# High halves of the activations straight from the transposes' bank; the first unit of a stage multiplied contraction block by contraction block

## The reference

```
h = x * (1.0 + sc_m) + sh_m          # per column scale and shift
z = h @ w_in                         # even / odd mixer: 1024 x (thousands)
x = layer_norm(ALPHA * x + (1.0 + g_m) * y, ...)
h = x * (1.0 + sc_f) + sh_f
u = causal_dwconv(h @ w_up, conv_w)  # w_up: 1024 x 5632
y = (silu(gate) * val) @ w_down
```

## Time and profile before

| what | value |
|---|---|
| median of 3 runs | 1254.31 us (1252.47 to 1254.63) |
| profiled execution, its own time | 1247.78 us |
| its span, first to last instruction | 1245.7 us |
| TensorE busy | 1155.2 us (93%), mean granted clock 0.965 |
| GpSimd busy | 827.4 us (66%) |
| ScalarE busy | 582.8 us (47%) |
| VectorE busy | 559.4 us (45%) |

### The profile page before, as it was taken

One profiled execution on the slowest core, in us unless ns is written; L12 is line 12 of the kernel. 1 busy time (PEld: TensorE's weight loads), 2 busy tenths in 40 slices (PEclk: granted clock), 3 DMA queues, 4 the chain that ended last, 5 costly groups with the idle time before them and its releaser, 6 DMA issues.

```text
span 1245.7 us, 21662 instructions
## 1 busy us (share of the span) xinstructions
PE 1155.2 (93%) x8119; PEld 1043.1 (84%) x8119; DVE 559.4 (45%) x1149; ACT 582.8 (47%) x868; POOL 827.4 (66%) x290
## 2 busy tenths in 40 slices
PE   6899798999999876999999989999999998999996
PEld 2799687999996873989999959999998987999995
DVE  4359666766557886375322372224211234111113
ACT  0443525554542435354554515455777543554452
POOL 3567448988882730689888825656565765988884
PEclk9899989999998988999999998999999998999998
DMA  9788567999984350678655523444444553666661
GB/s 342 262 292 231 187 209 233 345 335 320 301 301 151 98 136 1 220 227 263 202 179 175 170 65 93 144 135 137 136 139 136 187 165 103 194 192 183 188 185 67
DMA packets 253193, 237.69 MB, mean 191 GB/s; under 512 B 18043, under 2 KB 216496, under 8 KB 253136
## 3 DMA queue, kind: packets, MB, share of 16 engines
q1 hardware_dynamic: 237312, 202.80, 52.6%
q10 hardware_dynamic: 14784, 31.98, 7.1%
q0 software_dynamic: 1040, 2.12, 0.5%
HBM read 235.83 MB, written 1.05 MB: 190 GB/s over the span
## 4 chain that ended last, share of the span: by engine, by line
PE 72%; DVE 8%; ACT 7%; POOL 5%; DMA 5%; issue 2%; SPq 0%; DVEq 0%; POOLq 0%; ACTq 0%
PE bank L1147 18%; PE bank L1148 18%; PE bank L1149 18%; POOL unit_lo L688 5%; ACT unit_hi L790 3%; DMA raw<-in_ev_w_in 2%; PE bank L1186 2%; PE bank L1172 2%; PE bank L1174 2%; PE bank L1218 2%; PE bank L1206 1%; DMA att<-in_ada_w 1%; PE bank L1208 1%; PE bank L1226 1%; PE bank L1327 1%
## 5 line engine op out<-in xcount | busy, mean ns | idle before, releaser
L688 POOL TENSOR_TENSOR unit_lo<-raw,unit_hi 128x2048 fp32r<-128x2048 f32 (+4 forms) x88 | 349.3, 3973 | 261.0 <-ACT unit_hi L790 260.9
L1147 PE MATMUL bank<-h_hi,unit_hi 128*128 128x256 f32 x1248 | 354.2, 284 | 0.3
L1148 PE MATMUL bank<-h_lo,unit_hi 128*128 128x256 f32 x1248 | 353.5, 283 | 0.0
L1149 PE MATMUL bank<-h_hi,unit_lo 128*128 128x256 f32 x1248 | 353.4, 283 | 0.0
L722 POOL TENSOR_TENSOR unit_lo<-raw,unit_hi 128x2048 fp32r<-128x2048 f32 (+1 forms) x70 | 257.2, 3675 | 70.5 <-ACT unit_hi L922 66.9
L1147 PEld LDWEIGHTS bank<-h_hi,unit_hi 128*128 128x128 f32 x1248 | 239.6, 192 | 5.0 <-issue 1.3
L1148 PEld LDWEIGHTS bank<-h_lo,unit_hi 128*128 128x128 f32 x1248 | 239.6, 192 | 2.7
L1149 PEld LDWEIGHTS bank<-h_hi,unit_lo 128*128 128x128 f32 x1248 | 239.6, 192 | 0.0
L790 ACT ACTIVATE unit_hi<-raw 128x2048 fp32r<-128x2048 f32 (+4 forms) x98 | 163.2, 1666 | 105.9 <-PE bank L1149 38.0
L725 POOL TENSOR_TENSOR down<-raw_down,down 128x1024 fp32r<-128x1024 f32 x70 | 176.2, 2517 | 0.0
L1862 DVE SCALAR_TENSOR_TENSOR work<-bank,cols,work 128x254 f32<-128x254 f32 (+1 forms) x176 | 72.7, 474 | 146.9 <-ACT work L909 146.9
(11 more groups left out here) (310 smaller groups left out, 2065.1 us busy)
## 6 DMA issues: line engine op xcount, KB each, us to landing
raw<-in_ffn_w_up SPq DMA_DIRECT2D x88, 512.0 KB, 5.2
raw<-in_w_in SPq DMA_DIRECT2D x60, 512.0 KB, 4.6
raw_down<-in_ffn_w_down SPq DMA_DIRECT2D x44, 512.0 KB, 4.9
raw<-in_w_up SPq DMA_DIRECT2D x64, 256.0 KB, 3.1
raw_down<-in_w_down SPq DMA_DIRECT2D x32, 512.0 KB, 3.5
raw<-in_ev_w_in SPq DMA_DIRECT2D x28, 512.0 KB, 5.3
ada<-in_ada_w ACTq DMA_DIRECT2D x13, 1024.0 KB, 7.8
att<-in_ada_w SPq DMA_DIRECT2D x12, 1024.0 KB, 7.7
```

Source lines behind the costliest of these rows:

```text
L688: nc.gpsimd.tensor_tensor(ul[g % 2][:, w], raw[g % 2][:, w], uh[g % 2][:, w].bitcast(F32), ALU.subtract).then_inc(lo_up, 1)
L1147: nc.tensor.matmul(o, sh, mh, start=first, stop=False)
L1148: nc.tensor.matmul(o, sh, ml, start=False, stop=False)
L1149: return nc.tensor.matmul(o, sl, mh, start=False, stop=last)
```

## The change

- ScalarE writes hh directly from the banks, one kt block at a time, in the order 0 to 7, and counts `h_hi` up after each. It no longer touches hf. For the odd quarters it waits until VectorE has read the bank.
- VectorE writes hf of all four quarters, in the order 1, 0, 3, 2; for the even ones it waits until ScalarE has read the bank. It then subtracts only quarter 3 (in stage 0 all four, as before).
- GpSimd subtracts the quarters 0, 1 and 2, in that order, each behind VectorE's hf and ScalarE's hh. Its queue is otherwise unchanged.
- `first_units` multiplies the first unit of a stage block by block: for each kt, as soon as its hh is there, all column blocks (or row blocks) with the high and the low half of the weights; then for each kt the hl products. It waits for the unit's low half before it starts, except in stage 0 (`low_last`), where the low half comes last. In stage 4 it takes `G_F` and the first query unit together, in stage 5 the first two feed-forward blocks together.
- `keep_warm(8)` ahead of stage 2's transposes becomes `keep_warm(5)`.

```diff
             def h_low(n):
-                for q in (0, 2):
-                    pool.wait_ge(h_hi, 4 * n + q + 1)
+                for q in range(3):
+                    evacuated(pool, ("ht", n, q))
+                    pool.wait_ge(h_hi, KD * n + 2 * q + 2)
                     k = slice(2 * q, 2 * q + 2)
                     nc.gpsimd.tensor_tensor(hl[:, k, :], hf[:, k, :], hh[:, k, :].bitcast(F32), ALU.subtract
-                                            ).then_inc(h_lo[0], 1)
+                                            ).then_inc(h_lo_pool, 1)
...
             def h_high(n, columns, scale, shift):
                 evacuated(act, columns)
-                def whole(q):
+                for q in range(4):
                     o = full(act, ("ht", n, q))
+                    if q % 2:
+                        evacuated(act, ("ht", n, q))
                     for i in range(2):
                         kt = 2 * q + i
-                        dst, src = hf[:, kt, :], o[:, S * i:S * (i + 1)]
+                        dst, src = hh[:, kt, :], o[:, S * i:S * (i + 1)]
...
-                    ins.then_inc(free(("ht", n, q)), 1)
-                def high(q):
-                    evacuated(act, ("ht", n, q))
-                    k = slice(2 * q, 2 * q + 2)
-                    nc.scalar.activation(hh[:, k, :], hf[:, k, :], ACT.Copy).then_inc(h_hi, 1)
-                whole(1)
-                high(0)
-                high(1)
-                whole(3)
-                high(2)
-                high(3)
+                        ins.then_inc(h_hi, 1)
...
+            def h_low_ready(n, kt):
+                q = kt // 2
+                if n == 0:
+                    pe.wait_ge(h_lo_dve, q + 1)
+                elif q < 3:
+                    pe.wait_ge(h_lo_pool, 3 * (n - 1) + q + 1)
+                else:
+                    pe.wait_ge(h_lo_dve, 4 + n)
+
+            def first_units(n, gs, rows=False, low_last=False):
+                parts = []
...
+                if not low_last:
+                    for g in gs:
+                        pe.wait_ge(lo_up, g + 1)
...
+                for kt in range(KD):
+                    pe.wait_ge(h_hi, KD * n + kt + 1)
+                    for part in parts:
+                        multiply(part, kt, uh, hh, start=kt == 0 and part[3] == 0)
+                        if not low_last:
+                            multiply(part, kt, ul, hh)
+                for kt in range(KD):
+                    h_low_ready(n, kt)
+                    for part in parts:
+                        last = kt == KD - 1 and not low_last
+                        mm = multiply(part, kt, uh, hl, stop=last and ends(part))
+                        if last:
+                            final(part, mm)
+                if low_last:
+                    for g in gs:
+                        pe.wait_ge(lo_up, g + 1)
+                    for kt in range(KD):
+                        for part in parts:
+                            mm = multiply(part, kt, ul, hh, stop=kt == KD - 1 and ends(part))
...
-                up(0, 0, ready=h_ready((1, 3, 5)[f]), high=h_high_ready((1, 3, 5)[f]))
-                up(0, 1)
+                if f < 2:
+                    first_units((1, 3)[f], [g0])
+                    up(0, 1)
+                else:
+                    first_units(5, [g0, g0 + 1])
                 downward(0, 0, True, False)
...
-            for g in G_QI:
-                unit_cols(g, hh, hl, ready=h_ready(0), high=h_high_ready(0))
+            first_units(0, G_QI[:1], low_last=True)
+            unit_cols(G_QI[1], hh, hl)
...
-            keep_warm(8)
+            keep_warm(5)
             transpose_rows(2, x, 3)
-            for g in G_Z:
-                unit_rows(g, hh, hl, ready=h_ready(2), high=h_high_ready(2))
+            first_units(2, G_Z[:1], rows=True)
+            for g in G_Z[1:]:
+                unit_rows(g, hh, hl)
...
-            unit_cols(G_F, hh, hl, blocks=(0,), ready=h_ready(4), high=h_high_ready(4))
+            first_units(4, [G_F, G_QKV[FOX][0]])
             for j, g in enumerate(G_QKV[FOX]):
+                if j == 0:
+                    continue
...
             def h_columns(n, scale, shift):
-                for q in (0, 2):
-                    whole(q)
-                for q in (0, 1, 2, 3) if n == 0 else (1, 3):
-                    low(q)
+                for q in (1, 0, 3, 2):
+                    if q % 2 == 0:
+                        dve.wait_ge(h_hi, KD * n + 2 * q + 2)
+                    whole(q)
+                for q in range(4) if n == 0 else (3,):
+                    evacuated(dve, ("ht", n, q))
+                    dve.wait_ge(h_hi, KD * n + 2 * q + 2)
+                    k = slice(2 * q, 2 * q + 2)
+                    V.tensor_tensor(hl[:, k, :], hf[:, k, :], hh[:, k, :].bitcast(F32), ALU.subtract
+                                    ).then_inc(h_lo_dve, 1)
```

More of the change, by code:

```diff
@@ L1155, in unit_begin, with unit_cols @@
                 return bank[4 + g % 2]
-            def unit_cols(g, mh, ml, blocks=(0, P), ready=None, part=None, high=None):
+            def unit_cols(g, mh, ml, blocks=(0, P), ready=None, part=None):
                 o = bank[4 + g % 2] if part else unit_begin(g)
@@ L1168, in unit_cols @@
                         if ready and i == 0:
-                            pe.wait_ge(*(high or ready)(kt))
+                            pe.wait_ge(*ready(kt))
                         a = slice(slot(g) + kt * n + c, slot(g) + kt * n + c + P)
@@ L1172, in unit_cols @@
                             nc.tensor.matmul(o[:, 0:S], uh[s][:, a], mh[:, kt, :], start=kt == 0, stop=False)
-                            if not high:
-                                nc.tensor.matmul(o[:, 0:S], uh[s][:, a], ml[:, kt, :], start=False, stop=False)
+                            nc.tensor.matmul(o[:, 0:S], uh[s][:, a], ml[:, kt, :], start=False, stop=False)
                         else:
@@ L1178, in unit_cols @@
                     if i == 0:
-                        for kt in range(nkt if high else 0):
-                            pe.wait_ge(*ready(kt))
-                            a = slice(slot(g) + kt * n + c, slot(g) + kt * n + c + P)
-                            nc.tensor.matmul(o[:, 0:S], uh[s][:, a], ml[:, kt, :], start=False, stop=False)
                         pe.wait_ge(lo_up, g + 1)
@@ L1188, in unit_cols, with unit_rows @@
                     mm.then_inc(bank_full[4 + s], 1)
-            def unit_rows(g, sth, stl, ready=None, order=None, part=None, high=None):
+            def unit_rows(g, sth, stl, ready=None, order=None, part=None):
                 o = bank[4 + g % 2] if part else unit_begin(g)
@@ L1206, in unit_rows @@
                             nc.tensor.matmul(c, sth[:, kt, t], uh[s][:, a], start=i == 0, stop=False)
-                            if not high:
-                                nc.tensor.matmul(c, stl[:, kt, t], uh[s][:, a], start=False, stop=False)
+                            nc.tensor.matmul(c, stl[:, kt, t], uh[s][:, a], start=False, stop=False)
                         else:
@@ L1211, in unit_rows @@
                     if tt == 0:
-                        for kt in order if high else ():
-                            pe.wait_ge(*ready(kt))
-                            nc.tensor.matmul(c, stl[:, kt, t], uh[s][:, slot(g) + kt * n:slot(g) + kt * n + n],
-                                             start=False, stop=False)
                         pe.wait_ge(lo_up, g + 1)
@@ new lines, in first_units, with multiply, final, ends @@
+            def first_units(n, gs, rows=False, low_last=False):
+                parts = []
+                for g in gs:
+                    o, w = unit_begin(g), units[g].get("n", UC)
+                    for i in range(TT if rows else w // P):
+                        parts.append((g, o[:, w * i:w * (i + 1)] if rows else o[:, S * i:S * (i + 1)], w, i))
+                if not low_last:
+                    for g in gs:
+                        pe.wait_ge(lo_up, g + 1)
+                def multiply(part, kt, weight, h, start=False, stop=False):
+                    g, o, w, i = part
+                    a = slot(g) + kt * w
+                    if rows:
+                        return nc.tensor.matmul(o, h[:, kt, P * i:P * (i + 1)], weight[g % 2][:, a:a + w], start=start, stop=stop)
+                    return nc.tensor.matmul(o, weight[g % 2][:, a + P * i:a + P * (i + 1)], h[:, kt, :], start=start, stop=stop)
+                def final(part, mm):
+                    g, _, w, i = part
+                    if i == (TT if rows else w // P) - 1:
+                        mm.then_inc(bank_full[4 + g % 2], 1)
+                def ends(part):
+                    return part[3] == (TT if rows else part[2] // P) - 1
+                for kt in range(KD):
[12 more added lines that the diff above has]
+                if low_last:
+                    for g in gs:
+                        pe.wait_ge(lo_up, g + 1)
```

(6 more changed lines are left out.)

26 lines of the change are left out of this document (3 added, 23 removed).

## The result

| | before | changed |
|---|---|---|
| median of 16 runs each | 1251.5 us (1245.7 to 1256.1) | 1260.4 us (1252.9 to 1263.2) |
| ratio, changed to before | | 1.0062, 95% interval 1.0045 to 1.0080 |
| profiled execution, its own time | 1247.78 us | 1260.25 us |
| its span | 1245.7 us | 1258.1 us |
| mean granted clock | 0.965 | 0.962 |

The changed kernel is slower, by 7.8 us (5.6 to 10.0) as the ratio has it; the two medians are 8.9 us apart. I forecast 1260.0, and +5.7.

A forecast was written before the change was run, and what follows sets the result against it. TensorE, busy 93% of the span, was taken to bound the kernel. Terms 0.4 + 2.75 - 1.4 + 2.75 + 1.9 - 0.7 = +5.7 us on 1254.3 gave 1260.0 us, range 1250.0 to 1264.5.

The forecast's parts named there:

- Stages 1 and 3: Second unit's start: GpSimd's low half 1.0 us later, plus 1.75 for the lower clock after 3.5 us idle; +2.75 each.
- Stage 2: Five fillers start the transposes 2.56 us earlier, but VectorE's restoring sets the end: statistics 1.4 us earlier, -1.4.
- a sign of being wrong: Stage 2: the forecast is wrong if the statistics come more than 2.5 us early.
- the path: Stage 2's restoring: VectorE's passes alternate with GpSimd's work, so only 1.25 us of the 2.56 is gained there.
- Stage 5: First down product starts 1.1 us earlier, the third block's later low half takes back 0.4; -0.7.
- Stage 4: Forget unit's bank fills later, so ScalarE's next high copy and the units after are late; +1.9, bounds +0.9 and +7.
- Stage 0: Subtractions start later and end in the way of the second unit's low half; +0.4, bounds 0 and +2.
- Rival A: Clock holds before the second units of stages 1 and 3; both terms 1.0, sum +2.2, 1256.5 us; chance 0.20.
- Rival B: Head start kept: second unit before B+10.13, stages 1 and 3 gain 2.6 each, stage 2 4.0; 1246.7 us; chance 0.18.
- rival C: Lower clock also in stages 4 and 5, stage 0 on its bad side: +1.1, +1.7, +1.6 more; 1264.4 us; chance 0.12.

The follow-up runs named there:

- e11: Changed kernel with three filler products between the first and second unit of stages 1 and 3: 1250.8 us (one run).
- e6: Changed kernel with keep_warm(8) instead of keep_warm(5) ahead of stage 2's transposes: 1264.4 us, ratio to before 1.0082.
- e7: Changed kernel with stage 4's forget gates alone as first unit and the query unit behind, as before: 1259.7 us, ratio to before 1.0055.
- e1: Changed kernel with stage 0 alone as it was before: 1255.7 us, ratio to before 1.0012.
- e10: Changed kernel with the fifth unit's load held until the fourth's has landed: 1259.9 us (one run).
- e2: Changed kernel with the compare in VectorE's top-k tail written to a PSUM bank instead of SBUF: 1254.2 us, ratio to before 0.9997.
- e3: Kernel before with the top-k compare written to a PSUM bank instead of SBUF: 1248.4 us, ratio to before 0.9950.
- e4: Changed kernel with GpSimd's low half of the second unit ahead of its three subtractions in stages 1 and 3: 1249.9 us, ratio to before 0.9971.
- e8: Changed kernel with low halves ahead (stages 1, 3), top-k compare through a bank, chunk mask as the index sum's start value: 1246.9 us, ratio to before 0.9963.
- e12: As e8, with stage 0 in the old order and GpSimd's two gate-row loads moved behind the sixteenth unit's low half: 1246.0 us, ratio to before 0.9949.

## Why the prediction came true, and where it did not

**Stages 1 and 3** (+2.75 each): right in each step, and by its mechanism. The second unit started at B+11.0 (forecast 11.15), the wait was 3.3 us (3.5) and put down to GpSimd, and a stretch at 0.50 followed. Stage 3 measured +2.13: 1.45 for the clock (I had 1.75), 0.7 for the start (1.0, since three subtractions took 4.25 us together and the low half behind them 4.55). In stage 1 the clock stayed down for some 6 us, and e11 puts its price at 2.2 to 2.5. Cut at the normalisation of stage 2 (the row of 410.28 above), stage 1 takes 203.1 to 203.8 us in the three profiles of before and 205.7 to 206.7 in six of the changed order: +3.0 on the mean, a little under the later start and the clock together.

**Stage 2** (-1.4): the number was met partly by luck. From normalisation to statistics it took 28.3 us in the changed order and 30.90 in the profile from which I forecast (397.62 to 428.52). That is 2.6 us early, over the 2.5 that I had named as a sign of being wrong. But the other two profiles of before took 28.96 and 28.97; the second of them all:

```profile
399.70 1.54 DVE L1735 TENSOR_SCALAR x<-x,small 128x1024 f32<-128x1024 f32 x2 [0.61 <-POOL small L702]
...
428.66 0.23 DVE L2048 TENSOR_SCALAR small<-small 128x2 f32<-128x2 f32 x1
```

Against these the gain is 0.65, and 1.3 on the mean of the three. The first had run its filler in 9.97 us, the others in 8.77 and 8.51. The step that failed is the path: I let GpSimd's turns keep 1.2 us of a shift of 2.56. The three fillers shift the start by 1.6 and are worth 1.40 (e6); the new order of the activations costs 0.7 of that (29.71 in e6 against 28.96 and 28.97, eight fillers each), with the four restoring passes at 12.8 us instead of 11.8. By the means of the stretches, stages 1 and 2 are +1.0 together (0.6 and 0.4), where I had +1.35. **Stage 5** (-0.7): the stretch says -0.6.

**Stage 4** (+1.9): the copy was late, by 2.5 us (B+11.0 instead of 8.5; forecast 2.0, though a dozen matmuls at 0.213 and sixty at 0.12 end at 758.2, not the 757.9 I wrote, which makes it 2.3), but the term was not there at the end, about +0.4 with a scatter of 3. I took the delay of one unit through to the end of the path by a single wait for a load; e7 shows it all but used up by the eighth copy.

**Stage 0** (+0.4) is the term that failed in size. The rest sums to about +3 (0.6, 0.4, 2.1, 0.4, -0.6 by the stretches), so of the 7.8 us some 5 are stage 0's; e1 gives 4.7 to 6.3, and the means of the stretch (165.5 over seven profiles, 159.7 over three) 5.8. Shown are two ways: the fourth unit's high half starts 22.7 to 23.2 us after the first bank read instead of 21.0 to 21.5 (I had counted 0.4 of that, GpSimd's subtraction behind VectorE's), and the top-k tail met GpSimd more often. Not shown: why the load lands 1.3 us later (not by the fifth load, e10), whether the meeting follows from that delay or is chance, and how the loss divides between the two (e2 and e3 leave it open). My bounds for this term, 0 to +2, were too tight: I priced only the instructions that the change touches, not those behind a delay.

So the sum of 5.7 is near 7.8 partly by luck: 4.5 too little in stage 0, some 2.4 too much in stages 1 to 4. That 1260.0 met 1260.4 also rests on the median of three runs of before, 2.8 us over that of sixteen. Rival A would have been stage 3 at +0.7, as e11 built it. Rival B's condition, a second unit before B+10.1, is what e4, e8 and e12 made true, but not at B's price of 2.6 us a stage: against before, stage 3 took 0.2 us more in e4, 0.9 less in e12 and 2.0 less in e8, and stage 1, cut as above, some 0.6 less. Of rival C the worse stage 0 came true, the rest not.

## What to carry to other kernels

When one engine gets ahead, ask first which engine it then waits for: reordering that engine's queue took 5.9 us off the two stages that it touches, and with it the kernel went from 0.6% over the one before to 0.3% under (4.6 us of that untraced). A wait on TensorE can cost the delay and then the lower clock behind it, here some 1.1 to 1.45 us on top of 0.7 in stage 3; a few filler products of the right length pay the clock's part back. Profile the kernel before more than once: a local row of it moved by 1.9 us between profiles, which is more than the term that I read from it. And before a small term is called nothing, look for what downstream shares a port or a queue with another engine: in six of seven profiles with stage 0 changed, an instruction of 0.29 or 0.43 us stood under a lock of 3.7 to 4.7, in one of three with it old.

## What the runs showed of the hardware

- A VectorE TENSOR_SCALAR from SBUF to SBUF stands still until GpSimd's subtraction is over: 128x256 took 3.71 to 4.01 us instead of 0.29. My text said that an instruction with one SBUF input does not; that is wrong for this one. Written to a bank it took 0.43 us and was never held up. The Trainium skill has the exception that I left out ("SBUF — State Buffer", Who interferes with whom): in the modes that use both ports a one-input instruction takes the shared one too. The trace fits that: alone, 256 columns took 0.29 us SBUF to SBUF and 0.43 to a bank.
- The clock can fall without one long stop, and the waits alone do not tell when. Behind waits of 0.93 and 0.49 us it fell in stage 3 of e4 and held in stage 3 of e12 and in stage 1 of e4, e8 and e12; behind one of 0.90 it held in e8.
- Two stops of 3.29 us were not alike: the lower clock lasted 3.4 us in stage 3 and over 6 in stage 1.
- Two DMA queues shared by packets, not by bytes: 4.4 KB packets against 1.05 KB ones.
